# Routing weights cut into bf16 pieces by VectorE in two portions, and PSUM sums opened with four matmuls in place of twelve

## What is computed

```python
def moe_ffn(x, prm):                        # x: 544 tokens x 1024
    scores = sigmoid(xt @ prm['w_router'])  # 128 experts
    _, idx = lax.top_k(scores + prm['b_router'], TOP_K)        # 8 of them
    sel = jnp.take_along_axis(scores, idx, axis=-1)
    gate = sel / jnp.sum(sel, axis=-1, keepdims=True) * ROUTED_SCALE
    ...
    h = silu(xb @ prm['w_e1'][e]) * (xb @ prm['w_e3'][e])      # per expert, 1024 -> 256
    yb = (h @ prm['w_e2'][e]) * w[:, None]                     # 256 -> 1024, times gate
    acc.at[tok].add(yb)
    shared = (silu(xt @ prm['w_s1']) * (xt @ prm['w_s3'])) @ prm['w_s2']
    return shared + routed
```

## Time and profile before

| | us |
|---|---|
| median of 3 runs | 1860.45 |
| the runs | 1858.18, 1860.45, 1860.71 |
| the profiled execution | 1855.98 |
| its span | 1854.2 |
| TensorE busy | 1796.3 (97%) |
| VectorE busy | 896.3 (48%) |
| GpSimd busy | 349.1 (19%) |
| DMA, mean | 277 GB/s |

### The profile page before, as it was taken

The page is one execution under the profiler, slowest core; times in us unless marked ns, Lnnn a source line. Parts: engine busy times, 40 slices in busy tenths (PEclk is TensorE's granted clock), DMA queues, the critical chain, the costliest instruction groups (busy, mean ns, idle before and its releaser), DMA issues.

```text
span 1854.2 us, 36147 instructions
## 1 busy us (share of the span) xinstructions
PE 1796.3 (97%) x13858; PEld 1141.7 (62%) x13858; DVE 896.3 (48%) x1994; ACT 377.8 (20%) x836; POOL 349.1 (19%) x470
## 2 busy tenths in 40 slices
PE   8999998989999999699999999999999999999997
PEld 6877778878888875455555555554555555555452
DVE  0487745545544113545545454454545444555554
ACT  1114544431301002211111111111111111111113
POOL 1000003888800000211111111111111111111110
PEclk9999999999999999899999999999999999999999
DMA  5443212012423125479999999999999999999996
GB/s 159 166 159 108 75 35 54 5 40 69 163 91 114 68 95 195 174 284 419 419 420 421 419 419 420 419 420 420 417 419 420 413 416 418 416 411 420 420 418 241
DMA packets 109316, 513.53 MB, mean 277 GB/s; under 512 B 28150, under 2 KB 31478, under 8 KB 59038
## 3 DMA queue, kind: packets, MB, share of 16 engines
q1 hardware_dynamic: 84028, 478.34, 64.5%
q0 software_dynamic: 20544, 32.85, 4.9%
q10 hardware_dynamic: 4642, 0.91, 0.3%
HBM read 511.47 MB, written 41.48 MB: 298 GB/s over the span
## 4 chain that ended last, share of the span: by engine, by line
PE 84%; DMA 12%; issue 1%; DVE 1%; ACT 1%; POOLq 0%; POOL 0%; SPq 0%; DVEq 0%
PE bank L2158 20%; DMA arena<-in_w_e 12%; PE bank L2191 10%; PE bank L1432 10%; PE bank L2060 7%; PE bank L490 6%; PE bank L1113 5%; PE bank L1439 5%; PE bank L461 4%; PE bank L1983 3%; PE bank L2093 3%; PE bank L2009 2%; PE bank L452 1%; PE bank L2071 1%; PE bank L478 1%
## 5 line engine op out<-in xcount | busy, mean ns | idle before, releaser
L2158 PE MATMUL bank<-arena 128*64 128x256 f32 x4096 | 456.1, 380 | 9.2 <-DMA arena<-in_w_e 8.3
L2158 PEld LDWEIGHTS bank<-arena 128*64 128x64 f32 x4096 | 292.2, 137 | 184.1 <-issue 32.9
L2191 PE MATMUL bank<-arena 128*64 128x512 f32 x1024 | 247.9, 605 | 0.0
L2060 PE MATMUL bank<-arena 128*128 128x512 bf16 x792 | 203.3, 379 | 3.7 <-DVE arena L2471 1.8
L1432 PE MATMUL bank<-arena 128*128 128x276 f32 x768 | 182.6, 396 | 0.0
L1432 PEld LDWEIGHTS bank<-arena 128*128 128x128 f32 x768 | 145.7, 190 | 32.3
L1953 POOL DMA_INDIRECT arena<-h_rows,index x66 | 66.9, 1014 | 504.9 <-PE bank L2093 479.6
L2501 DVE TENSOR_TENSOR arena<-bank,arena 128x256 f32<-128x256 f32 x64 | 27.2, 426 | 260.7 <-ACT arena L2304 260.7
L1969 POOL DMA_INDIRECT routed_rows<-arena,index x64 | 78.9, 1232 | 385.2 <-ACT arena L2308 376.6
L2191 PEld LDWEIGHTS bank<-arena 128*64 128x64 f32 x1024 | 62.1, 136 | 127.4 <-issue 100.2
L2060 PEld LDWEIGHTS bank<-arena 128*128 128x128 bf16 x792 | 67.4, 98 | 105.8 <-issue 55.7
(11 more groups left out here) (351 smaller groups left out, 2204.4 us busy)
## 6 DMA issues: line engine op xcount, KB each, us to landing
arena<-in_w_e SPq DMA_DIRECT2D x384, 1024.0 KB
arena<-in_w_in SPq DMA_DIRECT2D x50, 512.0 KB, 3.6
arena<-routed_rows SPq DMA_DIRECT2D x5, 1024.0 KB, 15.0
arena<-in_w_mem_kv SPq DMA_DIRECT2D x4, 1024.0 KB, 5.8
arena<-in_cache_mem_k SPq DMA_DIRECT2D x8, 512.0 KB, 4.5
arena<-in_cache_mem_v SPq DMA_DIRECT2D x8, 512.0 KB, 5.3
arena<-in_w_out SPq DMA_DIRECT2D x2, 2048.0 KB, 12.6
arena<-routed_rows SPq DMA_DIRECT2D x8, 512.0 KB, 5.5
```

The lines of the kernel that those rows point to most:

```text
L2060: mm = pe.matmul(final_bank(t, h)[:, :], spread[:, v, t, :], parts[:, x, h * 512:(h + 1) * 512], start=first and x == 0, stop=last and x == 2)
L2158: mm = pe.matmul(p_gu[t * S:(t + 1) * S, x * DE:(x + 1) * DE], xt[:, v, c, t * S:(t + 1) * S], w13[2 * v + t][:, x, c, :], start=(c == 0), ...
L2191: mm = pe.matmul(p_y[t * S:(t + 1) * S, :], hidT[:, j, t * S:(t + 1) * S], w2[2 * v + t][:, j, h * 512:(h + 1) * 512], start=(j == 0), sto ...
```

## The change

The pieces are no longer made by GpSimd, whose whole loop is gone. VectorE makes them by a new function `cut(experts, rest)`, four operations with three drains, for all five tiles at once: the first portion (experts 0 to 3, `2 * AHEAD`) right behind the first `one_hot`, the remainder (124 experts) behind `shared_product(1, 0)`. The scratch of the first portion is `sel`; that of the second is `score` itself. TensorE's first `find_slots` waits for the first portion (`first_weights`), the second has no wait of that kind. SyncE's load of w2s waits for the second portion (`weights_cut`). The four banks are opened by one matmul each, with `spread[:, 1]`, zeroed by VectorE, as the stationary and 512 columns of the one-hot as the moving operand; the wait for the zeroed `parts` goes to where `parts` is first used, and the zeroing of `spread[:, 1]` moves ahead and now carries s_yv's first count.

```diff
@@ SyncE
         for v in range(2):
             sp.wait_ge(s_in[v], 16)
+        sp.wait_ge(sem("weights_cut"), 1)
         sp.dma_start(w2s, io["w_s2"][0].rearrange("(k p) n -> p k n", p=P)).then_inc(sem("shared_down_loaded"), 16)
@@ GpSimd
-        for i in range(NTT):
-            pool.wait_ge(sem("weights_scaled"), i + 1)
-            pool.tensor_copy(info[:, i, 0:NE, 2], score[:, i, :])
-            pool.drain()
-            pool.tensor_tensor(score[:, i, :], score[:, i, :], info[:, i, 0:NE, 2], ALU.subtract)
-            pool.drain()
-            pool.tensor_copy(info[:, i, 0:NE, 3], score[:, i, :])
-            pool.drain()
-            pool.tensor_tensor(info[:, i, 0:NE, 4], score[:, i, :], info[:, i, 0:NE, 3], ALU.subtract)\
-                .then_inc(sem("weight_pieces"), 1)
-        pool.drain()
-        pool.tensor_copy(info[:, :, NE:NEP, :], info[:, :, 0:NEP - NE, :]).then_inc(sem("weight_pieces"), 1)
@@ TensorE
-        pe.wait_ge(sem("weight_pieces"), NTT)
+        pe.wait_ge(sem("first_weights"), 1)
         find_slots(0, 0, 0)
         shared(0, 1)
-        pe.wait_ge(sem("weight_pieces"), NTT + 1)
         find_slots(1, 1, 1)
         shared(1, 1)
         pe.wait_ge(s_rc, NTT)
-        for h in range(2):
-            pe.wait_ge(s_part[h], 1)
-            for t in range(SUMMED):
-                spread_rows(1, t, h, first=True)
+        pe.wait_ge(s_yv, 1)
+        for t in range(SUMMED):
+            for h in range(2):
+                pe.matmul(final_bank(t, h)[:, :], spread[:, 1, t, :], onehot[:, 1, 0:NTT - 1].rearrange("p a e s -> p (a e s)"),
+                          start=True, stop=False)
@@ VectorE
+        def cut(experts, rest):
+
+            dve.tensor_copy(info[:, :, experts, 2], score[:, :, experts])
+            dve.drain()
+            dve.tensor_tensor(rest, score[:, :, experts], info[:, :, experts, 2], ALU.subtract)
+            dve.drain()
+            dve.tensor_copy(info[:, :, experts, 3], rest)
+            dve.drain()
+            return dve.tensor_tensor(info[:, :, experts, 4], rest, info[:, :, experts, 3], ALU.subtract)
...
         one_hot(0, 0)
+        cut(slice(0, 2 * AHEAD), sel[:, 0:2 * AHEAD * NTT].rearrange("p (a n) -> p a n", a=NTT)).then_inc(sem("first_weights"), 1)
         one_hot(1, 1)
...
-        dve.sem_inc(s_yv, 1)
+        dve.memset(spread[:, 1], 0.0).then_inc(s_yv, 1)
         shared_product(1, 0, third(1), 2)
-        dve.memset(spread[:, 1], 0.0)
+        cut(slice(2 * AHEAD, NE), score[:, :, 2 * AHEAD:NE]).then_inc(sem("weights_cut"), 1)
+        dve.drain()
+        dve.tensor_copy(info[:, :, NE:NEP, :], info[:, :, 0:NEP - NE, :])
```

More of the change, by code:

```diff
@@ L2055, in base, with spread_rows @@
             mm.then_inc(s_bp, 1)
-        def spread_rows(v, t, h, first=False, last=False):
+        def spread_rows(v, t, h, last=False):
             for x in range(3):
                 mm = pe.matmul(final_bank(t, h)[:, :], spread[:, v, t, :], parts[:, x, h * 512:(h + 1) * 512],
-                               start=first and x == 0, stop=last and x == 2)
+                               start=False, stop=last and x == 2)
             return mm
@@ L2420, in weigh @@
             dve.drain()
-            dve.tensor_scalar(score[:, i, :], gated, scale[:, i:i + 1], None, ALU.mult).then_inc(sem("weights_scaled"), 1)
+            dve.tensor_scalar(score[:, i, :], gated, scale[:, i:i + 1], None, ALU.mult)
         dve.memset(counts[:, 0, :], 0.0)
```

## The result

Eight runs of each kernel, side by side: 1859.05 us before (1856.3 to 1860.71), **1843.11 us after** (1838.05 to 1852.48), a ratio of 0.992, 95% interval 0.9902 to 0.9938. The change makes the kernel faster by 0.8%. The profiled execution took 1841.66 us, with a span of 1839.8.

What follows compares the result with a forecast made beforehand. TensorE, 84% of the span, was held ahead of the pair loop by GpSimd's late pieces; 11.5 + 2.3 + 1.8 + 1.8 = 17.4, less 0.2, gave 17.2 us, so 1843.2 us, 8-in-10 range 1839.5 to 1848.

Steps and rivals of the forecast that it cites:

- Part 1: Ahead of the first find_slots: VectorE makes the first portion of pieces, so find_slots(0) starts 11.5 us earlier (10.9 to 11.9).
- rival (d): VectorE's two portions: drains stall as GpSimd's did while DMA traffic runs, making the kernel slower, 1867 us; 2%.
- Part 2: TensorE at shared(0, 1): only 1.6 us idle before, so the clock stays full, gaining 2.3 us.
- Rival (a): TensorE ahead of and into the first pair: the clock falls all the same, costing 6 us, 1849 us; 7%.
- Part 3: Opening the banks: four matmuls in place of twelve gain 1.8 us, and the wait of 1.8 us goes.
- Part 4: First gather: turn(0, 0) starts at 780.1, the first pair at 782.9, moving the loop's start by 17.4 us.
- rival (c): First gather becomes the bound, needing 1 to 5 us more: 1844 to 1848 us; the part above 1 us, 8%.
- Part 5: Pair loop: nothing waits for something timed elsewhere, so the end moves with the start, except for what Part 6 adds.
- Part 6: Second portion and SyncE's queue: portion 5.3 us, w2s runs into the weight stream by about 1 us; charged 0.2 (0 to 4).
- the 4.5 that the prediction names as a sign: Start of the weight stream: a first load over 4.5 us after the first pair's start means wrong in size.
- Rival (b): Second portion costs the upper price, weights_cut comes after the gate, first load 2 us later: 4 us, 1847.2 us; 11%.
- the 1 us that the prediction allows: Pair loop: the sum of idle time on the weights' DMA stays unchanged within 1 us.

Runs made afterwards that it cites:

- the second experiment: Kernel before, with GpSimd issuing the two DMAs that fill xg behind its pieces instead of ahead of them; 1850.08 us against 1858.22, ratio 0.9958.
- the first experiment: Kernel before, with the four-matmul opening alone, GpSimd still making the pieces; 1854.99 us against 1858.22, ratio of all runs 0.9994.

## Why the prediction was right, and where it was not

The median was 1843.11 for a predicted 1843.2. The mechanism came as foretold; that the number is met to 0.1 us is luck, as two misses of about 3 us cancel (see the sum). Step by step, from the traces:

- **Part 1**, 11.5 us: 11.57. The first portion took 1.1 us against 0.96, and VectorE could begin it 0.2 us sooner, as the first one_hot took 0.82 us and not 0.93 (the two measured 1.86 together where GpSimd works beside VectorE, and 1.83 in the kernel with the fill behind the pieces). The trace's releaser is VectorE's L2356, as foreseen. What I did not see is that the gain is mostly a drain's: the prediction read the 11.92 us as a stall, took it for a drain's only in rival (d), there as a property of drains under anyone's traffic, and the second experiment gave it its cause: GpSimd's own two DMAs. With the same traffic of others the drain took 0.73 us, and VectorE's six drains met no stall: the steps around them stand 0.07 to 0.08 us apart.
- **Part 2**, 2.3 us: find_slots(0) to find_slots(1) went from 4.99 to 2.71, 2.28 us. Before, the clock read 0.50 from 777 to 789, in and behind the 13.10 us of idle time, and shared(0, 1) took 5.01 us; here idle time was 1.54 us, the clock stayed at 1.00, and shared(0, 1) took 2.74. Shown by itself in the kernel with fifteen matmuls (2.26). Rival (a) did not come here. It came in part in the kernel with the early megabyte, one of six with the new order and the new opening, behind a turn that waited for its gather.
- **Part 3**, 1.8 + 1.8 us: from find_slots(1) to the opening 4.70 to 2.92, from the opening to the turn 2.59 to 0.65: 1.78 and 1.94. Shown by the first experiment (3.59 together). That it would cost 12.6 us not to have the new opening under the new order stands in the prediction only between the lines: it says what VectorE has to do ahead of the zeroing, but does not price it.
- **Part 4**: the turn started at 781.58 of a stage begun 1.69 us late, so at 779.9 by the prediction's clock (780.1). The gather was in time, so rival (c) did not come, but by little: one more megabyte made the turn wait 0.73 us.
- **Part 5**: the loop hangs on its start in both its parts; the last 50.8 us of the span behind the last pair's start are the same in both kernels.
- **Part 6** was the mis-sized term. I charged 0.2 us and the loop lost 1.44. The second portion took 1.41, 1.02, 1.43, 2.28 us where I had 1.2, 0.8, 1.2, 1.85: 6.35 in place of 5.3, inside my bounds (2.8 to 7.6). That put w2s at 3.58 us behind the first pair, not 2.4, and nearly all of its 2.5 us against the stream's start, where I had counted 1. The first weights were issued 5.40 us behind the first pair, past the 4.5 that the prediction names as a sign that it is wrong in size: that sign came. That the strided writes would cost more than writes side by side came out so: the last step, two inputs and a bf16 output written 12 bytes apart, took 2.28 us for 620 columns, where 640 side by side took 0.824. The step of 12 bytes alone does not give the price, as 620 columns cast at it took 1.41 us and 640 took 2.29. I let a gap of 0.25 us at 816 stand for slack. How 2.5 us of w2s come to 1.44 us of loop is not shown. Rival (b) was thus half true: its mechanism came, its size was 1.4 us and not 4. TensorE's waits for the weights' DMA, 8.3 us in all before and 9.1 after, stayed within the 1 us that the prediction allows.
- **The sum.** For the profiled execution I gave 1838.8, and it was 1841.66, 2.9 us more: 1.2 us from part 6 and 1.7 us from ahead of the stage, where the clock fell for a moment at 388 us, of which more below. Then I added 4.5 us from profiled execution to median, as in the three runs before; the changed kernel's median is 1.45 us above its profiled execution, 3.0 less. These two cancel by chance. The fairer measure is the gain: the difference of medians is 15.9 us, for a predicted 17.2, as the kernel before has a median of 1859.05 over eight runs, 1.4 us less than over the three on which I built.

What stays open: which part of the scatter of the changed kernel's runs (1838 to 1852 us) is the clock. The profiles hold one execution each.

## What to carry to other kernels

Before work is taken off an engine that looks too slow, see what its first instruction waits for: here a drain was held by the engine's own DMAs (11.92 us, and 0.73 without them), and an order of two lines alone gave 9.2 of 11.6 us at the first find_slots. When work moves to a busy engine, cut it in what the next consumer wants now and what it wants later, and check what stands behind the later part in program order on every engine (here the opening's old wait, 12.6 us, and a load of 1 MB, 1.4 us). Where a stream keeps the DMA queues full to the end (0.99 busy or more here), a megabyte belongs ahead of it, in a lull where nothing else waits for the queues: right ahead of the stream it cost 2.5 to 2.8 us, in the lull of the first gather 1.0 us. Its issue time mattered less here than whose bytes it stood in front of: with the stream issued 3.88 us behind the first pair, as before, but w2s just ahead of it, the loop still took 1004.76 us.

## What the runs showed of the hardware

A drain on GpSimd behind two DMAs of its own stood until about when they had landed (11.92 us of idle time; 11.80 where the slower of the two took 12.5 us to land), and 0.73 us without them.

GpSimd and VectorE were slower side by side in part of their work. With GpSimd at its pieces beside it, VectorE's L2417 took 729 ns in the mean, and 373 with GpSimd at a stand; GpSimd's second cast took 976 ns in the mean, and 690 where most of it ran with VectorE idle. Which operands it takes was not tried.

Short idle stretches of TensorE and the clock, as far as rows show them. In the kernel before the matmuls of L1113 at 388 us come behind 2.74 us of idle time, with the clock at 1.00; in the changed kernel behind 2.91 us, and the clock goes to 0.50 for 3.4 us. First before, then after:

```profile
388.13 2.59 PE L1113 MATMUL bank<-arena 64*64 64x64 f32 x81 [2.74 <-issue]
```

```profile
388.06 4.01 PE L1113 MATMUL bank<-arena 64*64 64x64 f32 x81 [2.91 <-issue]
```

That idle stretch has nothing to do with the change: it lies 300 us ahead of it, and ranged from 2.12 to 4.03 us over the thirteen profiles. There the clock held behind 2.12, 2.17, 2.58, 2.62 and 2.74 us and fell behind 3.06, 3.15, 3.48, 3.63, 3.76 and 4.03 us; behind 2.91 us it fell in the changed kernel's profile and held in that of the kernel with the early megabyte:

```profile
387.39 2.59 PE L1113 MATMUL bank<-arena 64*64 64x64 f32 x81 [2.91 <-issue]
```

So the length of the stretch does not decide alone. Ahead of find_slots the clock fell behind 2.83 us (the fill behind the pieces) and 2.84 us (twelve filling matmuls), for 3.4 us each; in and behind 8.5 us (one portion, the old opening) it was down for 10.2 us, and in and behind 13.1 us (before, the opening alone) for 13.7 us. The matmuls behind the stretch at 388 us took 1.42 us longer in this pair of profiles, most of the 1.69 by which the stage began later, so a stretch of about 3 us can part two profiled executions by that. The 1.54 and 1.53 us left ahead of find_slots in the changed kernel's two profiles did not cost it the clock, yet idle time in one piece is not all that matters: in the kernel with the early megabyte the clock fell to 0.50 for 3.4 us at 782.3, where TensorE had stood idle for 1.54, 0.73 and 0.69 us and was in a fourth stretch, of 0.83 us. It did not do so in the other five profiles of kernels with the new order and the new opening.

Casts from f32 to bf16 written 12 bytes apart: 620 columns 1.41 us, 640 columns 2.29 us on VectorE, 620 columns 2.32 us on ScalarE, against 0.428 us for 512 columns side by side. Why 5 x 124 takes less than 5 x 128 was not tried. In the kernel the two differ in one more thing: the 128 columns of all five tiles lie side by side in `score`, without a gap, and in `info` they do not, while the 124 have a gap in both.
